# A second output projection with one wide moving operand for seven of its eight tiles

## The reference

```python
h = post_norm(h, 0.5 * mods[2] * swiglu(modulate(h, mods[0], mods[1]), ffn1_up[l], ffn1_down[l]), ...)
y = (sigmoid(gs) * (y_sc @ w_sc) + sigmoid(gm) * (y_ml @ w_ml) + sigmoid(gd) * (y_da @ w_da)) @ w_o
h = post_norm(h, mods[5] * y, ln_g[l, 1], ln_b[l, 1])
h = post_norm(h, 0.5 * mods[8] * swiglu(modulate(h, mods[6], mods[7]), ffn2_up[l], ffn2_down[l]), ...)
```

## Time and profile before

| | us |
|---|---|
| median of 3 runs | 2346.27 (2345.84 to 2346.60) |
| the profiled execution | 2345.9 |
| its span, first to last instruction | 2344.1 |
| PE busy | 2321.7 (99%) |
| DVE busy | 1656.5 (71%) |
| ACT busy | 1035.0 (44%) |
| POOL busy | 193.8 (8%) |

### The profile page before, as it was taken

One profiled execution on the slowest core, in us unless ns is written; L12 is line 12 of the kernel. 1 busy time (PEld: TensorE's weight loads), 2 busy tenths in 40 slices (PEclk: granted clock), 3 DMA queues, 4 the chain that ended last, 5 costly groups with the idle time before them and its releaser, 6 DMA issues.

```text
span 2344.1 us, 35714 instructions
## 1 busy us (share of the span) xinstructions
PE 2321.7 (99%) x12926; PEld 2023.2 (86%) x12926; DVE 1656.5 (71%) x2778; ACT 1035.0 (44%) x1765; POOL 193.8 (8%) x186
## 2 busy tenths in 40 slices
PE   8999999999999999999999999999999999999998
PEld 5888889888888888898888898888898898999997
DVE  6898577457767655669885368886665767878876
ACT  5433224435556544363222264322245347756554
POOL 2111010000000000021110000111000000001220
PEclk9999999999999999999999999999999999999999
DMA  8788475332222322338783328776644433656654
GB/s 275 239 250 253 123 214 149 82 96 75 73 68 81 95 81 72 108 91 256 236 248 111 94 79 250 233 237 181 180 117 117 117 100 104 172 142 196 193 160 141
DMA packets 540058, 356.89 MB, mean 152 GB/s; under 512 B 15207, under 2 KB 490897, under 8 KB 539921
## 3 DMA queue, kind: packets, MB, share of 16 engines
q1 hardware_dynamic: 538472, 354.70, 51.9%
q10 hardware_dynamic: 1448, 0.38, 0.1%
HBM read 337.20 MB, written 17.83 MB: 151 GB/s over the span
## 4 chain that ended last, share of the span: by engine, by line
PE 92%; DVE 2%; ACT 2%; issue 1%; DMA 1%; SPq 1%; POOL 0%; DVEq 0%; ACTq 0%; POOLq 0%
PE ps L1101 25%; PE ps L1103 25%; PE ps L1102 25%; PE ps L1401 2%; PE ps L1402 2%; PE ps L1400 2%; PE ps L1114 1%; PE ps L1474 1%; PE ps L1193 1%; PE ps L1195 1%; PE ps L1194 1%; PE ps L1511 1%; PE ps L1116 1%; DVE w_lo L2349 1%; PE ps L1413 0%
## 5 line engine op out<-in xcount | busy, mean ns | idle before, releaser
L2349 DVE TENSOR_TENSOR w_lo<-raw,w_hi 128x1024 fp32r<-128x1024 f32 (+3 forms) x430 | 496.2, 1155 | 424.3 <-ACT w_hi L1617 419.1
L1617 ACT ACTIVATE w_hi<-raw 128x1024 fp32r<-128x1024 f32 (+3 forms) x430 | 423.4, 985 | 842.5 <-PE ps L1103 646.8
L1101 PE MATMUL ps<-u_hi,w_hi 128*128 128x512 f32 (+2 forms) x2176 | 777.2, 357 | 1.0 <-DVE w_lo L2349 0.9
L1103 PE MATMUL ps<-u_hi,w_lo 128*128 128x512 f32 (+2 forms) x2176 | 772.5, 355 | 0.0
L1102 PE MATMUL ps<-u_lo,w_hi 128*128 128x512 f32 (+2 forms) x2176 | 772.3, 355 | 0.0
L1101 PEld LDWEIGHTS ps<-u_hi,w_hi 128*128 128x128 f32 x2176 | 410.8, 189 | 60.2 <-issue 1.4
L1103 PEld LDWEIGHTS ps<-u_hi,w_lo 128*128 128x128 f32 x2176 | 410.7, 189 | 58.2
L1102 PEld LDWEIGHTS ps<-u_lo,w_hi 128*128 128x128 f32 x2176 | 410.9, 189 | 55.7
L2767 DVE SCALAR_TENSOR_TENSOR ada_acc<-ada_in_up,cs,ada_acc 128x512 f32<-128x512 f32 x378 | 281.2, 805 | 0.0
L1101 PE MATMUL ps<-g,w_hi 128*128 128x512 f32 (+1 forms) x572 | 206.7, 361 | 0.0
L1103 PE MATMUL ps<-g,w_lo 128*128 128x512 f32 (+1 forms) x572 | 203.8, 356 | 0.0
(11 more groups left out here) (394 smaller groups left out, 3677.2 us busy)
## 6 DMA issues: line engine op xcount, KB each, us to landing
raw<-in_ffn_up SPq DMA_DIRECT2D x150, 512.0 KB, 4.7
raw<-in_w_in SPq DMA_DIRECT2D x132, 512.0 KB, 3.8
ada_in_up<-in_w_ada SPq DMA_DIRECT2D x108, 512.0 KB, 4.6
raw<-in_ffn_down SPq DMA_DIRECT2D x67, 384.0 KB, 3.6
fold_out<-ada_acc SPq DMA_DIRECT2D x32, 512.0 KB, 3.4
fold<-fold_out SPq DMA_DIRECT2D x32, 512.0 KB, 5.4
raw<-in_ffn_down SPq DMA_DIRECT2D x42, 320.0 KB, 3.2
h<-in_ffn_up SPq DMA_DIRECT2D x22, 512.0 KB, 4.3
```

What stands on the lines that cost most here:

```text
L1101: pe.matmul(ps[bank][:, cols_of], wh, a_hi, start=a, stop=False)
L1103: m = pe.matmul(ps[bank][:, cols_of], wl, a_hi, start=False, stop=b)
L1617: act.activation(hi, whole, ACT.Copy).then_inc(hi_done, 1)
L2349: dve.tensor_tensor(lo, whole, hi.bitcast(F32), ALU.subtract).then_inc(lo_done, 1)
```

## The change

For seven of the projection's eight tiles (0 to 6) the rounded activations and their rest become one moving operand of 512 columns, as in the down projection; PE issues two matmuls for each k instead of three, and DVE adds both halves of the bank to `h`, in two instructions in place of one. `z_hi` and `z_lo` become views of one tensor at the same addresses. Tile 7 stays as it was. `paired_chunk` learns to wait for each k and to call something behind a k.

```diff
+PAIRED_TILES = {5: range(0, 7)}
...
-    z_hi = at("z_hi", [P, KD, TOK], F32R, region + 64 * KB)
-    z_lo = at("z_lo", [P, KD, TOK], F32R, region + 80 * KB)
+    z = at("z", [P, 2, KD, TOK], F32R, region + 64 * KB)
+    z_hi, z_lo = z[:, 0], z[:, 1]
...
-        def paired_chunk(r, slot, bank, ks, first, last):
+        def paired_chunk(r, slot, bank, a, ks, first=True, last=True, ready=None, after_k=None, then=None):
 
             pe.wait_ge(lo_done, r + 1)
             for n, k in enumerate(ks):
                 wh, wl = weight_tiles(r, slot, n)
-                pe.matmul(ps[bank][:, :].rearrange("p (s t) -> p s t", s=2), wh, g[:, :, k, SEG:TOK],
+                if ready is not None:
+                    pe.wait_ge(ready[0], ready[1] + n)
+                pe.matmul(ps[bank][:, :].rearrange("p (s t) -> p s t", s=2), wh, a[:, :, k, SEG:TOK],
                           start=(first and n == 0), stop=False)
-                m = pe.matmul(ps[bank][:, 0:SEG], wl, g[:, 0, k, SEG:TOK], start=False,
+                m = pe.matmul(ps[bank][:, 0:SEG], wl, a[:, 0, k, SEG:TOK], start=False,
                               stop=(last and n == len(ks) - 1))
-            m.then_inc(chunk_used, 1)
+                if n == len(ks) - 1:
+                    m.then_inc(chunk_used, 1)
+                if n == after_k:
+                    then()
...
             def part(e, i, cols_of, signal=chunk_used, ready=None, after_k=None, then=None):
+                if 4 * i + e in PAIRED_TILES.get(n, ()):
+                    paired_chunk(base + 4 * i + e, (base + e) % SPLIT, e, z, range(KD), ready=ready,
+                                 after_k=after_k, then=then)
+                    return
                 chunk(base + 4 * i + e, (base + e) % SPLIT, e, of(z_hi, z_lo, range(KD), cols_of), cols_of,
                       ready=ready, signal=signal, after_k=after_k, then=then)
...
             dve.wait_ge(ln_cent, KD * (n - 1) + centre_index(n, k) + 1)
             segs = seg_order(n)
+            if k in PAIRED_TILES.get(n, ()):
+                link(dve.scalar_tensor_tensor(h[:, k, LAT[1]], ps[bank][:, 0:SEG], gate[:, k, 1:2], h[:, k, LAT[1]],
+                                              ALU.mult, ALU.add))
...
-                add_branch(e, e, t0, d0 + e + 1, s0 + e)
+                add_branch(e, e, t0, d0 + e + 1, s0 + e, e in PAIRED_TILES.get(n, ()))
```

More of the change, by code:

```diff
@@ L1318, in part @@
                 if i in PAIRED.get(n, ()):
-                    paired_chunk(r, (base + q) % SPLIT, q // 4, ks, q % 4 == 0, q % 4 == 3)
+                    paired_chunk(r, (base + q) % SPLIT, q // 4, g, ks, q % 4 == 0, q % 4 == 3)
                     return
```

## The result

The kernel takes 2349.32 us with the change (median of 22 runs) against 2345.85 before (22 runs): +3.47 us, a ratio of 1.0015 with a 95% interval of 1.0009 to 1.0021. The forecast was +3.4. The two profiled executions are 2348.8 and 2345.9 us long; they differ by less than the medians, because PE reached the projection 0.74 us earlier in the profile after (2115.68 and 2116.42 us). L is 28.62 us before and 32.20 after, +3.58.

What follows compares the result with a forecast made beforehand. DVE, not the equally full PE, was taken to set the hand-over: PE's -0.75 us brings nothing, 7 x 0.52 - 0.21 = +3.4 us on DVE, so 2346.27 + 3.4 = 2349.7 us. Forecast range 2348.3 to 2350.8; 8 in 10, 2347.0 to 2351.0.

Steps and rivals of the forecast that it cites:

- What bounds the kernel: Projection stretch: PE and DVE both full, but DVE sets the time at the hand-over to the next stage, without slack.
- The change on PE: Projection, seven tiles: a pair takes 0.3467 us against 0.36 for three matmuls; PE saves 0.75 us, in front of waits.
- The change on DVE: Seven tiles: one more half-bank add each, waiting on itself, at 0.52 us; 0.39 kept for the range.
- Where the adds lie: DVE's order: 1.56 us late at the third sum, 1.35 at the centring after 0.21 idle, 3.43 after tile 6.
- The waits: PE stands 1.6 us before the pivot, then 2.0, 0.6 and 0.5 before the next stage's first three groups.
- Given back later: After the third group of the next stage: nothing gives the 3.4 us back.
- hidden: Rival: adds fit into DVE's waiting time, PE's saving shows, 2345.5 us; half hidden some 2347.5; 12 in 100 for both.
- a slow wide matmul: Rival: wide matmuls on the projection's operand run at twice the price per column, PE loses 13 us; 1 in 100.
- The clock: Rival: new PE waits bring its clock from 2.4 to 1.2 GHz behind the last, 2354.1 us; 6 in 100.

Runs made afterwards that it cites:

- adds_alone: Kernel before, narrow matmuls kept, plus one spare add of the same shape and wait for each of tiles 0 to 6; +4.03 us against before.
- wide_no_add: Changed kernel, wide matmuls on seven tiles, but DVE adds only the lower half of the bank; +0.19 us against before.
- spaced: Changed kernel with another DVE instruction moved between the two adds of tiles 0, 3, 4, 5 and 6; +2.25 us against before.
- pair_early: Changed kernel with only tiles 0 to 2 in the wide form; +1.54 us against before.
- centre_early: Kernel before, with DVE's centring of tiles 5, 6 and 7 moved in front of the add of tile 4; 2345.55 us against 2345.74, ratio 0.9998.

## Why the prediction was right

*What bounds the kernel:* right. The reading that PE is full and DVE is nonetheless ahead of it at the hand-over was what mattered; adds_alone and wide_no_add show each half by itself.

*The change on PE:* the price of a pair, 0.347 us, is what the changed kernel shows (2129.68 to 2130.03). That the saving brings nothing held: adds_alone, which lacks it, has the same L. Without the extra adds 0.13 us of it would go through the pivot (wide_no_add). With room on DVE in front of the hand-over it is 0.48 and not 0.75: the term was too large by the waits in tile 0 and at the pivot.

*The change on DVE:* 0.52 us for each pair, as in the earlier trace rows. The other price of the working, 0.39, is that of an add with another instruction between the two (spaced). The Trainium skill, "VectorE: DVE Perf Modes", section "The DRAIN you can't avoid", has it that a semaphore after each instruction of a chain costs nothing extra, measured there on eight copies; the rows differ from it here by 0.13 us for each add.

*Where the adds lie:* the third sum starts 11.60 us after the first matmul, against 9.93 before: +1.67, where 1.56 was forecast; 0.10 of it lies between the second sum and the split behind it (0.44 us and not 0.34 from start to start), which I can't explain. The idle time at the pivot swallowed 0.14 and not 0.21: where PE waits for the third sum, DVE still stands for 0.07 us until the pivot is taken and copied (the centring starts 1.20 to 1.21 us after the sum's end in all eight kernels where PE waits so). So DVE was +1.53 late at the centring (2128.91), where I had 1.35. Behind it come four adds of 0.51 to 0.52, as forecast, and the third split is at +3.58. What the working did not ask is which instructions GpSimd's additions would meet after the move. They are the same four as before, a sum of squares, two centrings and the first split, at the same lengths within 0.02 us; that was luck, as pair_early and wide_no_add (0.12 and 0.11 us) and spaced (0.55) show.

*The waits:* 1.6, 2.0, 0.6 and 0.5 us were forecast. By distances between starts less one pitch of 0.12 there are 1.69 (2125.95 to 2127.76), 1.87 (2140.40 to 2142.39), 0.56 and 0.43. The listed ones are 0.16 to 0.17 us shorter each. The 2.0 should have been 1.8 by the working's own prices: PE gains some 0.4 us behind the pivot (27 pairs at 0.0133) and not 0.5. Nothing in the sum hangs on it.

*Given back later:* nothing. The distance from the third group to the end of the span is 199.06 us before and 199.12 after.

*The rivals:* hidden fell with adds_alone; a slow wide matmul with wide_no_add. The clock did not fall behind the waits. The windows of PE after (length, busy PE, granted clock, DMA share, GB/s) are at 1.00, the level of 2.4 GHz, on both sides of the hand-over:

```profile
2115.68:2142.39 26.71, 23.46 (x141) 1.00 0.50 148
2142.39:2157.50 15.11, 14.09 (x110) 1.00 0.65 201
```

As a whole, +3.47 us (0.15%) was measured against +3.4 (2349.32 us against 2349.7, as the median before is 2345.85 by 22 runs and 2346.27 by the three that the forecast started from), within the 0.2% that the forecast called no change for a measurement of this kernel. The terms are a little less good than that: 0.18 us were missed at the pivot, and in the profile the sum is 3.58, where the working had 3.43.

## What to carry to other kernels

Where two engines are both full, an exchange of work between them is worth what the one that is late at the next hand-over gains or loses, and the other's saving is worth nothing as long as it waits there: the 0.75 us forecast for PE brought none, and the adds that DVE was given cost 3.6. Whether an engine is late is read from ends against starts: matmuls that begin 0.13, 0.05 and 0.05 us after a split ends, three times in a row before the change, say that there is next to no slack, although the list of waits shows hardly any idle time. An expected number that comes out is not yet its reason: centre_early came out near its forecast while DVE, which was to be out of the way, still set the hand-over. Such an edit is to be priced place by place: a tile that is followed by a pivot, a split or a hand-over has another price than one behind which the engine idles.

## What the runs showed of the hardware

VectorE and GpSimd hold each other up in this stretch, and which instruction pays depends on the order: two low halves take 0.87 or 1.84 us, a centring 0.41 or 0.96, one of GpSimd's additions 0.85 or 1.65. Moving an instruction out of the way mostly moved the loss to another. The adds that read a bank of PSUM are not touched: 0.47 us for the one at 2142.20 before, while GpSimd's instruction of 2141.22 ran to 2142.88. The Trainium skill, "SBUF — State Buffer", section "Who interferes with whom", says this of VectorE instructions with two inputs in SBUF beside a GpSimd instruction that reads SBUF, and excludes those with at most one; the rows agree with both parts. I had priced the seven new adds without it, and they were indeed free of it, but when their places changed (spaced) 0.55 us of such delays went.

The first matmul behind the wait in tile 0 is followed 0.10 us later than in a stream, whether wide (0.33 us and not 0.23) or narrow (0.22 and not 0.12). Behind the pivot it is 0.19 in both forms (0.42 and 0.31). Pairs ran at 0.347 us in most stretches, and at 0.353 in tile 0 of every kernel where it is wide and behind the pivot in wide_no_add and spaced; why is open.
